# A two-layer trunk on one core: the boundary between layers by token tile, and the conditioning matrix streamed through the mixing

## The reference

```python
for l in range(DEPTH):                                   # 2
    mod = silu(c) @ ada_w[l] + ada_b[l]                  # (1024) @ (1024 x 6144)
    sh1, sc1, g1, sh2, sc2, g2 = split(mod, 6)
    h = rms_norm(x, norm_mix_w[l]) * (1 + sc1) + sh1
    aq, ak, av, mqk, mv, mi, mf, mo, ga, gb = split_cols(h @ w_in[l])
    ya = sliding_window_attention(rope(norm(aq)), rope(norm(ak)), av, sinks[l]) @ w_attn_up[l]
    hm = mlstm_chunkwise(silu(conv(mqk)), mv, mi, mf)    # normalized per head
    yb = (sigmoid(mo) * hm) @ w_mlstm_up[l]
    x = x + g1 * ((sigmoid(ga) * ya + sigmoid(gb) * yb) @ w_out[l])
    h2 = rms_norm(x, norm_ffn_w[l]) * (1 + sc2) + sh2
    x = x + g2 * grouped_moe(h2)                         # 16 experts, top 2 of the best group
```

## Time and profile before

| | us |
|---|---|
| median of 3 runs | 1731.04 |
| lowest, highest | 1729.79, 1739.95 |
| span of the profiled execution | 1724.8 |
| PE / DVE / ACT / POOL busy | 1506.9 / 563.9 / 323.4 / 121.8 |
| mean granted clock of PE | 0.940 of full |
| DMA over the span | 366.59 MB, 213 GB/s |

### The profile page before, as it was taken

How to read it: one execution, slowest core, us unless ns; L and a number is a source line. 1 busy time by engine, 2 the same in 40 slices (tenths; PEclk the granted TensorE clock), 3 DMA queues, 4 the chain that set the end, 5 groups by cost and what they waited for, 6 DMA issues and landing times.

```text
span 1724.8 us, 18335 instructions
## 1 busy us (share of the span) xinstructions
PE 1506.9 (87%) x5819; PEld 669.3 (39%) x5820; DVE 563.9 (33%) x1459; ACT 323.4 (19%) x809; POOL 121.8 (7%) x157
## 2 busy tenths in 40 slices
PE   4999999999983999987749999999999387999982
PEld 1544444544441333332335444454444132333330
DVE  1346432446333212111134554243642411221213
ACT  3133411200011212111132343111000121221210
POOL 1100000011101000000111000000110100000001
PEclk8999999999996999999769999999999789999996
DMA  9822111055747899999952111113563799997984
GB/s 307 338 97 98 49 49 49 13 206 173 291 142 268 268 375 379 376 388 360 322 180 98 49 49 50 49 49 108 206 224 145 292 314 381 378 354 247 310 303 165
DMA packets 160813, 366.59 MB, mean 213 GB/s; under 512 B 12433, under 2 KB 14705, under 8 KB 160753
## 3 DMA queue, kind: packets, MB, share of 16 engines
q1 hardware_dynamic: 127568, 256.26, 42.2%
q0 software_dynamic: 21664, 83.89, 12.8%
q10 hardware_dynamic: 11520, 25.70, 5.0%
HBM read 334.37 MB, written 31.46 MB: 212 GB/s over the span
## 4 chain that ended last, share of the span: by engine, by line
PE 69%; DMA 11%; SPq 5%; DVE 5%; issue 4%; ACT 2%; POOL 2%; ACTq 0%; DVEq 0%; POOLq 0%; PEldq 0%
PE bank L939 23%; PE bank L1160 14%; PE bank L929 11%; PE bank L1105 6%; PE bank L1172 6%; DMA weight_ring<-in_w_up_dram 6%; DMA regA<-in_w_up_dram 2%; SPq L428 2%; SPq L431 2%; SPq L371 2%; DMA weight_ring<-in_ada_w_dram 1%; PE bank L1152 1%; PE bank L999 1%; POOL expert_rows L558 1%; PE bank L988 1%
## 5 line engine op out<-in xcount | busy, mean ns | idle before, releaser
L939 PE MATMUL bank<-h_features,weight_ring 128*128 128x512 f32 x768 | 342.4, 599 | 3.1 <-ACT regB L674 1.9
L1160 PE MATMUL bank<-weight_ring,merged_features 128*64 128x512 f32 x960 | 227.2, 628 | 35.3 <-DMA weight_ring<-in_w_up_dram 28.2
L939 PEld LDWEIGHTS bank<-h_features,weight_ring 128*128 128x128 f32 x768 | 144.8, 192 | 182.7 <-issue 182.4
L929 PE MATMUL bank<-weight_ring,h_features 128*128 128x512 f32 (+1 forms) x512 | 196.1, 541 | 1.7 <-ACT h_features L628 1.7
L1703 DVE TENSOR_TENSOR merged_features<-bank,merged_features 64x512 f32<-64x512 f32 x44 | 30.5, 693 | 381.8 <-ACT merged_features L809 381.8
L1160 PEld LDWEIGHTS bank<-weight_ring,merged_features 128*64 128x64 f32 x960 | 73.5, 144 | 165.4 <-issue 160.8
L929 PEld LDWEIGHTS bank<-weight_ring,h_features 128*128 128x128 f32 x512 | 96.0, 190 | 97.0 <-issue 91.6
L1160 PE MATMUL bank<-h_features,merged_features 128*64 128x512 f32 x256 | 117.1, 612 | 11.0 <-DMA regA<-in_w_up_dram 10.0
L1160 PE MATMUL bank<-regA,merged_features 128*64 128x512 f32 x256 | 117.5, 614 | 0.0
L1105 PE MATMUL bank<-weight_ring,merged_features 128*128 128x512 f32 x256 | 110.4, 593 | 3.0 <-POOL merged_features L538 3.0
L1172 PE MATMUL bank<-weight_ring,merged_features 128*64 128x512 f32 x480 | 109.6, 598 | 1.6 <-DVE merged_features L1689 1.6
(11 more groups left out here) (304 smaller groups left out, 1376.1 us busy)
## 6 DMA issues: line engine op xcount, KB each, us to landing
weight_ring<-in_ada_w_dram SPq DMA_DIRECT2D x24, 2048.0 KB, 8.7
weight_ring<-in_w_gate_dram SPq DMA_DIRECT2D x22, 2048.0 KB, 21.1
weight_ring<-in_w_down_dram POOLq DMA_DIRECT2D x22, 2048.0 KB, 14.9
weight_ring<-in_w_up_dram SPq DMA_DIRECT2D x22, 2048.0 KB, 20.4
weight_ring<-in_w_in_dram SPq DMA_DIRECT2D x18, 2048.0 KB, 8.9
h_features<-in_w_gate_dram SPq DMA_DIRECT2D x10, 2048.0 KB, 17.4
regA<-in_w_up_dram SPq DMA_DIRECT2D x10, 2048.0 KB, 27.4
regB<-in_w_down_dram POOLq DMA_DIRECT2D x10, 1536.0 KB, 11.5
```

The source lines that it names most:

```text
L929: ins = te.matmul(bank[:, 0:w], hT[:, k, P * i:P * i + P], wv[:, k, :], start=(k == 0), stop=(k == KD - 1))
L939: ins = te.matmul(bank[:, :], wv[:, k, c0:c0 + P], rhs[:, k, :], start=(k == 0), stop=(k == kn - 1))
L1160: ins = te.matmul(ps[3][64 * part:64 * part + 64, :], xT[:, k, :], w[:, k, :], start=(k == 0), stop=(k == KD - 1))
```

## The change

- **Layer boundary.** The meeting (`layer_end`, `share`) goes. SyncE alone clears the semaphores, in two sets: those of the mixing (`mix_sems`) once the four other engines have reached the experts (`mix_done`), those of the experts (`moe_sems`) in the next mixing, once they have left the experts (`moe_done`). An engine enters a mixing when `mix_cleared` allows it (`start_layer`), the experts when `moe_cleared` does (`start_experts`).
- **Normalized tokens** are transposed by token tile (`h1_transposes`), tiles 0 and 1 before `q` 0, tiles 2 and 3 between `q` 0 and `kv` 0, in banks 4 to 7; ScalarE evacuates four feature blocks of a tile, DVE the other four.
- **Gathers.** The two experts of a token are ordered by slot; the lower one's rows are gathered first, when all blocks through expert 14 are stored, the higher one's when all are. `combine` becomes two passes. The scatter goes in the order higher, lower. The gate weights are worked out behind the block tables.
- **Conditioning matrix.** Only slices 0 to 3 of layer 0 are still products. All others are summed on DVE (`sum_ada`), slices 4 to 11 of the layer and then 0 to 3 of the last layer ahead (`STREAM`; in layer 1 these four are done too and not used). The sums stand at the ends of DVE's steps 2, 4, ... 14, in turn 0 of `ga`/`ya`, and in turns 0, 2, 4, 6 of `yb`; PE reduces each after the group that `ADA_AT` names (`mod_sum`). The stream has one 2 MB buffer, in the space of `x`: `x` is stored to DRAM at the start of a mixing and fetched before `wo`.
- **Loads.** Slots are new. The next layer's q, kv, mqk0, mqk1, mv and mo are loaded at the end of the experts; for layer 0 they are issued after the head's sums, and SyncE opens layer 0 behind them. `params` of the next layer moves from the last experts to the routing. `w_down` of expert 1 is now in `regB`, that of expert 2 in the ring; 0 and 1 are loaded after `yb`, 2 after `wo`.
- PE waits for DVE's copy of the parameter columns before the head's products.

```diff
+STREAM = [(0, c) for c in range(HEAD_ADA, 12)] + [(1, c) for c in range(HEAD_ADA)]
+N_OWN = 8
+ADA_AT = {("mqk", 3): 0, ("mqk", 5): 1, ("mqk", 7): 2, ("mv", 1): 3, ("mv", 3): 4, ("mo", 1): 5, ("mo", 3): 6,
+          ("ya", 1): 7, ("yb", 1): 8, ("yb", 3): 9, ("yb", 5): 10, ("yb", 7): 11}
...
-        def layer_end(eng, l, mine):
-            eng.sem_inc(meet_a, 1)
-            wait_reg(eng, meet_a, l * 5 + 5)
-            for s in mine:
-                eng.sem_clear(s)
-            eng.sem_inc(meet_b, 1)
-            wait_reg(eng, meet_b, l * 5 + 5)
+        def start_layer(eng, l):
+            wait_reg(eng, mix_cleared, l + 1)
+        def start_experts(eng, l):
+            eng.sem_inc(mix_done, 1)
+            wait_reg(eng, moe_cleared, l + 1)
...
# SyncE, before the loop over layers
+            for j in range(1, HEAD_ADA):
+                load_head(j)
+            for name in ("q", "kv", "mqk0"):
+                load(0, name)
+            sp.wait_ge(head_sum, HEAD_ADA)
+            for name in ("mqk1", "mv", "mo"):
+                load(0, name)
+            sp.sem_inc(mix_cleared, 1)
# SyncE, in a layer
+                def load_ada(n):
+                    ahead, c_ = STREAM[n]
+                    src = cols8(ada_w, DEPTH - 1 if ahead else l, 512 * c_, 512)
+                    if n:
+                        sp.wait_ge(mid_ready, n)
+                    sp.dma_start(ada_w8[:, 1:KD, :], src[:, 1:KD, :]).then_inc(ada_in, 16)
+                    if 1 <= n <= N_OWN:
+                        through(sp, "ada", n - 1)
+                    sp.dma_start(ada_w8[:, 0:1, :], src[:, 0:1, :]).then_inc(ada_in, 16)
...
+                    wait_reg(sp, gu_ready, blocks_through(sp, E - 3))
+                    load(nxt, "q")
+                    load(nxt, "kv")
+                    wait_reg(sp, y_ready, blocks_through(sp, E - 2))
+                    load(nxt, "mqk0")
+                    wait_reg(sp, gu_ready, blocks_through(sp, E - 1))
+                    load(nxt, "mqk1")
+                    load(nxt, "mv")
+                    wait_reg(sp, y_ready, blocks_through(sp, E - 1))
+                    load(nxt, "mo")
...
# GpSimd
-                wait_reg(pool, y_out, nb * 32 + 32)
-                for i in range(NT):
-                    for k in range(2):
+                for k in range(2):
+                    wait_reg(pool, y_out, (nb if k else blocks_through(po, E - 2)) * 32 + 32)
+                    for i in range(NT):
...
# TensorE
+                def mod_sum(n):
+                    pe.wait_ge(mid_ready, n + 1)
+                    bank = take("ada", n)
+                    if STREAM[n][1] in (4, 5, 10, 11):
+                        ins = te.matmul(bank[:, :], ones[:, :], sum_buf(n), start=True, stop=True)
+                    else:
+                        ins = column_sums(bank, sum_buf(n))
+                    ins.then_inc(pj_ready, 1)
...
+                h1_transposes(0)
+                h1_transposes(1)
                 for i in range(NT):
+                    pe.wait_ge(h1_low, i + 1)
+                    pe.wait_ge(h1_high, i + 1)
                     token_group("q", i, 512)
+                    if i == 0:
+                        h1_transposes(2)
+                        h1_transposes(3)
                     token_group("kv", i, 256)
...
                         att_out(s - 6)
+                    name, i = ("mqk", s) if s < 8 else ("mv", s - 8) if s < 12 else ("mo", s - 12)
+                    if (name, i) in ADA_AT:
+                        mod_sum(ADA_AT[name, i])
...
# VectorE
+                def sum_ada(n):
+                    dve.wait_ge(ada_in, 32 * n + 32)
+                    acc = sum_buf(n)
+                    link(ve.tensor_scalar(acc, ada_w8[:, 0, :], cz[:, 0, 0:1], None, ALU.mult))
+                    for k in range(1, KD):
+                        link(ve.scalar_tensor_tensor(acc, ada_w8[:, k, :], cz[:, k, 0:1], acc, ALU.mult, ALU.add))
+                    ve.sem_inc(mid_ready, 1)
...
                 for s in range(16):
+                    prev = ("mqk", s - 1) if s < 9 else ("mv", s - 9) if s < 13 else ("mo", s - 13)
+                    if prev in ADA_AT:
+                        mod_chunk(ADA_AT[prev])
                     if s < 8:
                         conv(s)
...
+                    if s % 2 == 0 and s >= 2:
+                        sum_ada(s // 2 - 1)
+                mod_chunk(ADA_AT["mo", NT - 1])
...
+                    if ("ya", j) in ADA_AT:
+                        mod_chunk(ADA_AT["ya", j])
+                    if j == 0:
+                        sum_ada(7)
...
+                    if ("yb", j) in ADA_AT:
+                        mod_chunk(ADA_AT["yb", j])
+                    if j % 2 == 0:
+                        sum_ada(N_OWN + j // 2)
```

More of the change, by code:

```diff
@@ L34, with sums @@
 HEAD_ADA = 4
-G2_ADA = 10
-MID_ADA = {1: 4, 2: 5, 3: 6, 4: 7, 5: 8, 6: 9}
+STREAM = [(0, c) for c in range(HEAD_ADA, 12)] + [(1, c) for c in range(HEAD_ADA)]
+N_OWN = 8
+ADA_AT = {("mqk", 3): 0, ("mqk", 5): 1, ("mqk", 7): 2, ("mv", 1): 3, ("mv", 3): 4, ("mo", 1): 5, ("mo", 3): 6,
+          ("ya", 1): 7, ("yb", 1): 8, ("yb", 3): 9, ("yb", 5): 10, ("yb", 7): 11}
 def group_order(NT, NH, HM):
-    o = [("h1T", k) for k in range(8)]
+    def sums(name, i):
+        return [("ada", ADA_AT[name, i])] if (name, i) in ADA_AT else []
+    o = []
     for i in range(NT):
@@ new lines, in _ @@
+                through(sp, "q", NT - 1)
+                load(l, "ga0")
+                wait_reg(sp, moe_done, l * 4 + 4)
+                for done in moe_sems:
+                    sp.sem_clear(done)
+                sp.sem_inc(moe_cleared, 1)
+                load_ada(1)
+                load_ada(2)
+                through(sp, "mqk", 7)
+                load(l, "ga1")
+                load_ada(3)
+                load_ada(4)
+                through(sp, "mv", NT - 1)
+                load(l, "ya")
@@ L427, in load_gate @@
+                load_ada(5)
+                load_ada(6)
+                through(sp, "mo", NT - 1)
+                load(l, "yb")
+                load_ada(7)
+                load_ada(8)
+                through(sp, "ga", 3)
+                load(l, "gb0")
+                through(sp, "ga", 7)
+                load(l, "gb1")
                 def load_gate(p, e):
@@ L1303, in _ @@
                 head_norm(0, i)
-            head_mod(0)
+            head_cols(0)
+            ve.sem_inc(head_read, 1)
+            for j in range(HEAD_ADA):
+                dve.wait_ge(head_bc, j + 1)
+                hlink(ve.tensor_copy(modc[:, 4 * j:4 * j + 4], ps[2 + j % 2][:, 0:4]))
+                ve.sem_inc(head_read, 1)
+            head_mod(modc[:, 0:16])
+            dve.sem_inc(moe_done, 1)
             with dve.Fori(0, DEPTH) as l:
+                start_layer(dve, l)
                 n = [0]
@@ L1721, in _ @@
                     hn[0] = 0
[L1722 removed]
+                    head_cols(l + 1)
+                    head_mod(modn[:, :])
                     for i in range(NT):
[L1724 removed]
+                        combine(0, i)
+                    for i in range(NT):
+                        combine(1, i)
+                        ve.sem_inc(combined, 1)
                         if i:
@@ L1730, in _ @@
                     for i in range(NT):
-                        combine(i)
-                layer_end(dve, l, share(4))
+                        combine(0, i)
+                    for i in range(NT):
+                        combine(1, i)
+                        ve.sem_inc(combined, 1)
+                dve.sem_inc(moe_done, 1)
 def program(nc, args):
```

458 lines of the change are left out of this document (214 added, 244 removed).

## The result

| | before | after |
|---|---|---|
| median of 4 runs, us | 1730.41 | 1802.09 |
| lowest, highest | 1727.65, 1739.95 | 1797.5, 1805.44 |
| ratio (95% interval) | | 1.0408 (1.0372 to 1.0444) |
| span of the profiled execution | 1724.8 | 1799.6 |
| PE / DVE busy | 1506.9 / 563.9 | 1515.8 / 634.9 |

The change costs 71.7 us by the medians and 74.8 by the spans, where +44 was forecast. This table takes the spans apart at landmarks on PE: from each landmark to the next, after less before, and beside it the term of the sum.

A forecast was written before the change was run, and what follows sets the result against it. Attention steps were taken as bound by a chain through PE, DVE and ScalarE, experts partly by DMA. Terms 62 + 5 + 9.8 - 19 - 2 - 5.5 - 2 - 4 = +44 on 1724.8: span 1769, median 1775, range 1748 to 1796.

The forecast's parts named there:

- the price of TensorE's clock behind PE's waits: Attention steps: a long wait costs up to 2.8 us more in slow products; 2 us a layer added for three waits.
- The gap between the layers: Last combination to next layer's q: meeting and four head sums go, lower gathers start earlier; -19 us (-14 to -26).
- The steps: The 16 attention steps: seven sums on DVE make PE wait; 31 us a layer (25 to 38), +62 for two.
- The walk: Step-by-step estimate of PE and DVE through the attention steps with the sums: +28.9 us a layer before the clock's share.
- rival (3): Costs more: five waits a layer each pay 2.8 for the clock (+16), gathers wait for weights (+4): 1795 us; chance 0.10.
- The other sums: Sums 7 to 11, outside the attention steps: a 3.9 us wait before sum 8 plus PE's reductions; +5 for both layers.
- The rule of the shared port: Upper gathers: VectorE and GpSimd SBUF access exclude each other, up to 5 us more in the sum; judged not to apply.
- The row's 0.3 us: Upper gathers between the layers: issue beside DVE's combinations takes 1.21 us instead of 0.94, so 0.3 each.
- The start: Layer 0 entered only after six weight-load issues, q at 58.6 instead of 53.38, plus clock and transposes: +9.8 us (5 to 13).
- The experts: Parameters leave layer 0's saturated stretch, -2 us; w_down 1 loaded before the experts shortens layer 1's early DMA wait, -5.5.
- Routing and wo: Routing: seven operations of 0.2 us go behind the block tables, about 1 us a layer; -2 us.
- The end: End of the kernel: first gather at 1695.3, the eighth at 1704.1 instead of 1708.29; -4 us.

The follow-up runs named there:

- e1: Changed kernel with each of the seven attention-step sums cut to its first operation (wrong slices): steps 150.8 us in both layers, kernel 1772.7 us.
- e4: Changed kernel with the twelve sums moved to other places of DVE's program, PE's reductions at least a group behind, e2's buffers: 1759.0 us, ratio 1.0174.
- e5: e2 with DVE storing a reduction's result, which frees PE's bank, before it begins the next sum: 1776.8 us, ratio 1.0278.
- e2: Changed kernel with PE reducing most sums one group or turn later, and own buffers for sums 0 to 7: 1783.9 us, ratio 1.0306.
- e3: Changed kernel with next-layer mqk0, mqk1, mv, mo loaded after the last gather, layer 0 opened at the start, yb reductions a turn later: 1778.9 us.
- e7: Changed kernel with mqk0, mqk1, mv, mo of the next layer loaded only once its first h1 tile is evacuated: 1800.9 us, ratio 1.0408.
- e9: Changed kernel with expert 2's w_down loaded when the experts begin, as before the change, not after wo: 1803.8 us, ratio 1.0396.
- e8: e6 plus later yb reductions, layer 0 opened at the start, mqk0, mqk1, mv, mo loaded after the first h1 tile: 1720.1 us, ratio 0.9948.
- e10: e8 with expert 6's w_down issued only when expert 5's w_up has landed: 1715.4 us, ratio 0.9892 to the kernel before.
- e6: e4 with the sums of ga/ya turns 1 to 6 each split over two turns: 1741.9 us, ratio 1.0061.

## Why the prediction was wrong

The direction was right, and so was the mechanism of the attention steps. The sum was 31 us too small by the spans. The step that failed is the price of TensorE's clock behind PE's waits: the prediction put it at 2 us a layer in the attention steps and at nothing in the turns and in `wo`, and the runs show 7.5 and 9.9, some 4.6 and 1.7 a layer, about 26 us more in all. The gap between the layers and the preload of `w_down` failed beside it. Other terms erred the other way. One by one:

**The steps (+69.7, forecast 62).** The walk held: with the start 5.5 late, the changed kernel's steps 6, 8, 10, 12 and 14 began 8.3, 13.4, 18.0, 21.1 and 30.2 us later than before, where the walk has 7.7, 13.0, 17.6, 19.5 and 27.8; e1 and e4 ended within 1.5 us of it. Its waits were even too long, 21.5 for 18.8; a sum took 5.95 us and not 6.25, and the time before the reductions, put at some 25 us a layer, was 19.3. What was mis-sized is the clock: 2 us were added for three long waits, partly hidden; measured are 7.5 and 9.9 us of slower products and reductions. That the walk's delays and the term of 62 came this close is in part luck, since over both layers waits 6 us too long stand against a clock 13 us too cheap. The earlier trace rows gave 2.8 for one long wait, and rival (3) charged it at each of five waits a layer. It was said to decide below a mean clock of 0.9; the clock was 0.94 and 0.92, and the price came all the same. The threshold was guessed, not worked out: 138 us of products at 0.94 are by estimate already some 9 us too long. One more sign was missed. The prediction had every slice there in time, with sums 15 us or more apart; DVE was ready for sum 6 2.7 us behind the end of sum 5, and waited 5.5 and 5.7 us for its slice. It cost PE nothing here (its reduction at 275.95 had no wait), but it did in e5.

**The other sums (+16.4, forecast 5).** The waits were right (4.7 for 3.9). The clock was left out here altogether: 2 us in the 16 products behind sum 8 and 0.9 in its reduction. Another 0.8 lies in `ga` 0, which took 9.54 us instead of 8.73 (granted clock 0.74 for 0.81), and 0.8 in the small products ahead of it (0.83 for 0.98); what lowered the clock there was not tried. e2 and e3 took 7.5 us a layer out by reading sum 8 a turn later.

**Between the layers (-10.8, forecast -19).** Two terms. The combination ended 2.9 us later than forecast, counted from the last expert product: the last rows landed after 7.1 us with 404 GB/s on the DMA engines, where the forecast kept the store at its old time and charged the weights to the gathers alone. Then `q` was put 2.6 us behind the combination; it came 8.7 behind. In the chain this is ScalarE, which first normalizes the last tiles (4.5 us), goes back to the top of its loop (2.65) and evacuates h1 (1.5). DVE's own way back, 4.5 us, runs beside it and ends within half a us of it. The kernel before has that way too, and its chain shows it as issue, but it was not among the rows that I read:

```profile
877.31 3.32 issue
880.63 0.04 DVEq L1305
880.67 4.38 issue
885.04 0.06 DVE regU L1342
```

**The way back is a transfer.** With the DMA engines almost idle DVE needed 4.5 us and with 386 GB/s on them 7.8 (e3); with the loads moved behind it 4.6 (e7). The DMA views of these stretches, and of the one before's last row, list 4 to 8 packets of instruction queues (here e3's, 893 to 901 us). The Trainium skill ("Runtime: NRT & Kernel Launch", Instruction fetch mechanics) says that a taken branch to a page that is not at hand forces a DMA fetch of that page before the engine goes on. The runs agree; I had not looked for it. No run took the jump itself away, so how much of the 4.5 us is the fetch stays open.

```profile
q14 instruction: 4, 0.03, 1.9%
```

**The rule of the shared port.** Upper gathers took 1.56 to 1.83 us beside DVE's combinations, which looks like the rule of the Trainium skill ("SBUF — State Buffer", SBUF: two separate sides). At the end of layer 1, with 241 GB/s on the DMA engines, three combinations in a row ran from 1784.16 to 1788.08 us, and the gathers beside them:

```profile
1784.16 0.94 POOL L630 DMA_INDIRECT regA<-expert_rows,slot_index  x1 [2.96 <-DMA expert_rows<-merged_features]
1785.41 0.94 POOL L630 DMA_INDIRECT regA<-expert_rows,slot_index  x1 [0.30 <-issue]
1786.65 0.94 POOL L630 DMA_INDIRECT regA<-expert_rows,slot_index  x1 [0.30 <-issue]
```

An exclusion for the length of a combination does not fit this. But a loaded DMA alone does not explain the long gathers either. Between the layers the lower ones, with 399 GB/s and no combination beside them, took 0.94 to 1.00 us (898.01 above); the upper ones had the same 399 GB/s. Only where both came together were gathers long, and with e3's 326 GB/s it was the first upper one alone (1.70). How the two act together was not tried. The row's 0.3 us were too little there, the gathers took 0.6 to 0.9 us longer each.

**The start (+5.5, forecast 9.8).** `q` began at 57.2 (forecast 58.6), the gate behind six issues opened at 53.3 (54.4). The 2.4 for the clock did not come: the first products ran at full clock. e3 shows what the gate cost in all, 11.7 us, since without it `q` starts 8 us earlier than before.

**The experts (-0.4, forecast -7.5).** `w_down`: e9. The bytes were counted, but not whether the DMA engines were full where they lay: 215 GB/s in the 13.8 us behind layer 1's first gate_up. The wait that was to go stayed: block 5 began 71.0 us behind block 0, before 72.9. In e8 and e10 it is moved by what goes beside expert 5's `w_up`, some 20 us later. For the parameters 2 us were put, and layer 0's experts took 0.7 less.

**Routing and wo (+1.9, forecast -2).** The term itself held: from the router to the first gate_up 0.4 us are gained in layer 0 and 1.4 in layer 1. But from `wo` to the router lie 69.2 us after against 67.3 before, in both layers, and 1.7 of these are in the products of `wo`. PE waits 1.5 us before them in both kernels, yet the granted clock of the first 4 us is 0.59 after and 1.00 before (windows of after and of before):

```profile
489.80:494.00 4.20, 4.20 (x6) 1.81 (x7) 0.00 (x0) 0.00 (x0) 2.20 (x3) 0.59 0.99 361
```

```profile
442.40:446.50 4.10, 4.10 (x10) 1.95 (x11) 0.17 (x1) 0.00 (x0) 2.21 (x3) 1.00 0.96 344
```

e4 to e6 ran `wo` as before in both layers, e2 and e8 in one of the two. Why the clock falls behind this wait in some layers and not in others was not tried.

**The end (-7.5, forecast -4).** The last gathers landed after 6.3 us instead of 7.6, and the first four were through early.

**The range.** The median, 1802, lies 6 us above it. Its upper end, 1796, took one adverse case at a time. Three stretches (the steps, the turns of `ga`/`ya` and `yb`, `wo`) had the same thing too small or left out, the clock behind a wait, and came out high together; the bounds of each were added as if they were independent.

## What to carry to other kernels

Work that an idle-looking engine takes over is free only if its step still fits in the other's step; where two engines already release each other in a circle, a walk of a few steps gives the delay within some us. Price every wait of PE of over 2 us with the slow products behind it (behind a wait of 1.5 us it came in some layers and not in others), and put the reader of a result a turn behind its maker, with its bank freed before the next long piece of work. Ahead of a point where everything waits for a small transfer (rows, gathers, the way back to a loop's top), keep large loads back: they had 45 us of room here, up to the first mqk group.

## What the runs showed of the hardware

- **Clock behind short waits.** Waits of 2.4 to 2.8 us already made the next 8 products 4.7 to 5.2 us long instead of 3.6 (e4, granted clock 0.76 to 0.68). A wait of 4.7 us cost 2 us in the next 16 (0.78). Behind a wait of 1.5 us the first 4 us of `wo` ran at 0.59 in the changed kernel and at 1.00 in the kernel before and in e4.
- **Code over DMA.** Back to a loop's top: DVE 4.5 us and ScalarE 2.7 with DMA nearly idle, 7.8 and 5.5 under 386 GB/s.
- **Two queues share.** GpSimd's 2 MB `w_down`, issued while SyncE's `w_up` was under way, belongs to a landing of 41.8 us instead of 36.3 once held back (e8, e10). The Trainium skill ("DMA: Bandwidth & Descriptors", Queues, rings and completion order) has each DMA engine take turns between the queues that have work, which the two runs agree with. Why layer 1's second block took 7.1 us in the changed kernel and in e9 and 8.8 to 9.6 in the others, the kernel before among them, I did not settle.
